# A feed-forward whose panels begin with a product made in two column pieces

## The reference, cut to what matters

```python
def swiglu(x, w_gate, w_up, w_down):
    return (jax.nn.silu(x @ w_gate) * (x @ w_up)) @ w_down

h = h + 0.5 * swiglu(rmsnorm(h, ffn1_norm[l]), ffn1_w_gate[l], ffn1_w_up[l], ffn1_w_down[l])
h = h + hybrid_mixer(rmsnorm(h, mix_norm[l]), ...)
h = h + 0.5 * swiglu(rmsnorm(h, ffn2_norm[l]), ffn2_w_gate[l], ffn2_w_up[l], ffn2_w_down[l])
```

## Time and profile before

| what | value |
|---|---|
| median of 3 runs (lowest, highest) | 2210.49 us (2203.68, 2211.15) |
| profiled execution | 2210.91 us |
| its span | 2209.1 us |
| PE busy | 2198.0 us, 99%, 18114 matmuls |
| PEld busy | 2180.8 us, 99%, 18114 loads |
| DVE busy | 1602.4 us, 73% |
| ACT busy | 1276.6 us, 58% |
| DMA | 386.68 MB, mean 175 GB/s |

### The profile page before, as it was taken

One profiled execution on the slowest core, in us unless ns is written; L12 is line 12 of the kernel. 1 busy time (PEld: TensorE's weight loads), 2 busy tenths in 40 slices (PEclk: granted clock), 3 DMA queues, 4 the chain that ended last, 5 costly groups with the idle time before them and its releaser, 6 DMA issues.

```text
span 2209.1 us, 48942 instructions
## 1 busy us (share of the span) xinstructions
PE 2198.0 (99%) x18114; PEld 2180.8 (99%) x18114; DVE 1602.4 (73%) x2450; ACT 1276.6 (58%) x1988; POOL 282.1 (13%) x328
## 2 busy tenths in 40 slices
PE   8999999999999999999999999999999999999999
PEld 8999999999999999999999999999999999999999
DVE  6655997665566579887768767888768766777775
ACT  6444786544444368766546646876556645565662
POOL 0001661100100136220020012010010010101000
PEclk9999999999999999999999999999999999999999
DMA  6555435555455544455555555355556645445553
GB/s 229 174 188 165 159 122 170 167 171 195 155 173 183 179 161 144 144 185 186 190 169 193 195 183 163 124 178 194 195 181 200 219 162 177 161 162 194 188 200 124
DMA packets 100408, 386.68 MB, mean 175 GB/s; under 512 B 11312, under 2 KB 12464, under 8 KB 100304
## 3 DMA queue, kind: packets, MB, share of 16 engines
q1 hardware_dynamic: 99648, 383.89, 52.2%
q0 software_dynamic: 368, 1.26, 0.2%
q10 hardware_dynamic: 288, 0.12, 0.0%
HBM read 384.18 MB, written 1.05 MB: 174 GB/s over the span
## 4 chain that ended last, share of the span: by engine, by line
PE 98%; ACT 1%; DVE 1%; issue 0%; DMA 0%; ACTq 0%
PE bank L387 16%; PE bank L389 15%; PE bank L388 15%; PE bank L395 15%; PE bank L396 14%; PE bank L397 14%; PE bank L759 1%; PE bank L1049 1%; PE bank L1050 1%; PE bank L1051 1%; PE bank L1096 0%; PE bank L709 0%; PE bank L740 0%; PE bank L940 0%; PE bank L943 0%; PE bank L942 0%
## 5 line engine op out<-in xcount | busy, mean ns | idle before, releaser
L412 DVE TENSOR_TENSOR wlo<-raw,whi 128x1024 fp32r<-128x1024 f32 (+1 forms) x677 | 893.3, 1322 | 177.8 <-ACT whi L405 165.4
L405 ACT ACTIVATE whi<-raw 128x1024 fp32r<-128x1024 f32 (+1 forms) x677 | 745.5, 1112 | 164.5 <-PE bank L389 117.2
L387 PE MATMUL bank<-u,whi 128*128 128x272 f32 (+1 forms) x1888 | 549.0, 291 | 7.1 <-DVE u L450 7.1
L389 PE MATMUL bank<-u,wlo 128*128 128x272 f32 (+1 forms) x1888 | 543.7, 288 | 0.0
L388 PE MATMUL bank<-u,whi 128*128 128x272 f32 (+1 forms) x1888 | 541.9, 287 | 0.0
L395 PE MATMUL bank<-u,whi 128*128 128x256 f32 x1888 | 529.2, 280 | 0.2
L397 PE MATMUL bank<-u,wlo 128*128 128x256 f32 x1888 | 527.4, 279 | 0.0
L396 PE MATMUL bank<-u,whi 128*128 128x256 f32 x1888 | 527.4, 279 | 0.0
L387 PEld LDWEIGHTS bank<-u,whi 128*128 128x128 f32 x1888 | 356.9, 189 | 8.0 <-DVE wlo L412 7.3
L388 PEld LDWEIGHTS bank<-u,whi 128*128 128x128 f32 x1888 | 357.0, 189 | 0.9 <-issue 0.2
L397 PEld LDWEIGHTS bank<-u,wlo 128*128 128x128 f32 x1888 | 357.6, 189 | 0.0
(11 more groups left out here) (332 smaller groups left out, 3448.8 us busy)
## 6 DMA issues: line engine op xcount, KB each, us to landing
raw<-w SPq DMA_DIRECT2D x552, 512.0 KB, 3.4
raw<-w SPq DMA_DIRECT2D x128, 704.0 KB, 4.1
h<-xT SPq DMA_DIRECT2D x4, 272.0 KB, 4.9
outT<-h SPq DMA_DIRECT2D x8, 128.0 KB, 4.7
consts<-cst POOLq DMA_DIRECT2D x1, 576.0 KB, 4.6
dist<-cst POOLq DMA_DIRECT2D x1, 192.0 KB, 2.7
rdist<-cst POOLq DMA_DIRECT2D x1, 192.0 KB, 3.0
sgain<-small POOLq DMA_DIRECT2D x1, 145.5 KB, 4.8
```

Source lines behind the costliest of these rows:

```text
L387: pe.matmul(out, w_h, x_hi, start=first, stop=False)
L389: return pe.matmul(out, w_l, x_hi, start=False, stop=last)
L405: act.activation(whi[:, n % RING, 0:COLS[n]], raw[:, n % RING, 0:COLS[n]], ACT.Copy).then_inc(hi_ready, 1)
L412: dve.tensor_tensor(wlo[:, n % RING, 0:COLS[n]], raw[:, n % RING, 0:COLS[n]], whi[:, n % RING, 0:COLS[n]], ALU.subtract).then_inc(lo_ready, 1)
```

## The change: what it does

In the gate and up panels of the five feed-forwards with 256 tokens, the first matmul of a panel (k = 0, high by high) is made as two, over columns 0 to cut and cut to 256, with the same weights. The first piece has `start=True`, the second has not. `CUTS` gives the column for each j of a step and each phase. For y = 5 and j = 0 it is 0, and there the matmul stays whole. Nothing else is changed: the columns that are computed, the banks, the waits and all other engines' instructions are the same.

```diff
+CUTS = {5: (0, 128, 64, 192), 7: (224, 32, 240, 16), 9: (248, 8, 252, 4), 10: (208, 48, 96, 160),
+        12: (250, 244, 254, 220)}
...
-        def split_products(pe, out, slot, k, x_hi, x_lo, first, last):
+        def split_products(pe, out, slot, k, x_hi, x_lo, first, last, cut=0):
...
-            pe.matmul(out[:, 0:SEQ], w_h, x_hi, start=first, stop=False, skip_group_check=True)
+            if cut:
+                pe.matmul(out[:, 0:cut], w_h, x_hi[:, 0:cut], start=first, stop=False, skip_group_check=True)
+                first = False
+            pe.matmul(out[:, cut:SEQ], w_h, x_hi[:, cut:SEQ], start=first, stop=False, skip_group_check=True)
...
                                 mm = split_products(pe, bank[g % 4], n % RING, k, u_at(uy, 0, k),
-                                                 u_at(uy, 1, k), k == 0, k == KD - 1)
+                                                 u_at(uy, 1, k), k == 0, k == KD - 1,
+                                                 CUTS[y][j] if k == 0 else 0)
```

## The result

The changed kernel takes 2221.09 us (median of 4 runs, 2220.36 to 2221.74). The kernel before, in the same comparison, takes 2207.09 us (2203.68 to 2211.15). The ratio is 1.0064, with a 95% interval of 1.0044 to 1.0083: slower, by 0.6%. Two of the four runs of before lie at 2203.68 us and two at 2210.49 and 2211.15, so its median falls between two levels; against the upper one, where the profiled execution lies, the change costs 10 us. I had forecast 2242 us. The profiled execution took 2220.83 us where that of before took 2210.91, so the two traces have 9.9 us between them to explain; 31.2 were forecast. The direction was right, the size was three times too large.

The account below looks back on a forecast made before the run. PE was taken to bound the kernel, with matmuls and weight loads busy for 99% of the span. The sum was 2210.9 + 22.5 (pairs) + 8.7 (pitch) = 2242 us, range 2220 to 2250.

Parts of the forecast that it names:

- (1) Number: In the five feed-forwards' gate and up panels, 209 split panels add 209 matmuls and 209 weight loads.
- (2) Price of a pair: Per split panel, two pieces take 2 x 0.112 us against 0.118 for one wide matmul: +0.106, 22.5 us in all.
- The load rows: Profile rows of narrow matmuls in rt: one weight load every 0.11 us, read as the pace of any narrow piece.
- rivals C and D: C, chance 0.04: second piece's load skipped or hidden, 2220 us; D, 0.03: also fast pitch in slow feed-forwards, 2190 us.
- (3) The pitch behind the pieces: In the five feed-forwards, pieces set the pitch anew, 0.85 of the matmuls at the slow one: +8.7 us.
- seven passages: Places in rt behind narrow matmuls; six of seven ran slow, from which the slow share of 0.85 was taken.
- rival B: Pieces turn nearly every panel of the five feed-forwards to the fast pitch, 2212.5 to 2221 us; chance 0.11.
- (4) Waits: At the split panels no wait is added or moved; the bank's handover 0.11 us later is hidden by three others.
- Rival E: Pieces cost their price but each feed-forward keeps its pitch, 2233 us; chance 0.27 together with mixtures of pitch.

## Why the prediction was wrong

What bounds the kernel: right. PE never waits, and every ns per matmul shows in the total; all twelve runs agree with it.

(1) Number: right, 18323 matmuls.

(2) Price of a pair: forecast 0.106 us each and 22.5 us in all; measured 24.9 in the trace and 0.115 us each in the run with 220 more pairs. The load rows gave the right mechanism: the width of a piece doesn't matter and equal weights are loaded again. It was 10% low: I had set two pieces at 112 ns each against one wide matmul at 118, but in the fast stream two at 113 stand against one at 113, and behind some cuts come a few matmuls of transition. So rivals C and D, which need the load skipped or hidden, fall. The Trainium skill, page TensorE: Matmul & The Clock Gate, section Back-to-back issue gap, says that in a stream of weight loads and matmuls both set the time from one matmul to the next, and gives about 81 ns for 128 columns and 131 ns for 512. The traces agree that the load counts, as 4 columns take 113 ns, but not with the figures: 128 columns take 111 ns, and 512 columns in rt (L1049 to L1051) start about 230 ns apart.

(3) The pitch behind the pieces: this step failed. I forecast +8.7 us and the runs showed -14.1: 20% of the feed-forward matmuls are at the slow pitch (1056 + 528 of 7920) where I took 85%. I had seen rightly that there are two pitches, what each is worth, and that pieces turn them and the stream keeps them. I took the share from seven passages as if they were seven draws. Four of them were one piece of code, L1082: six matmuls of 256 columns, 118 ns apart each time, and then six of 128, which is nearer to one observation than to four. I had left out the five norms, which set the pitch too, three slow and two fast. And the run with cut 8 shows that the way of a turn depends on what ran ahead. With a share of 0.5 for want of knowledge the sum would have been 22.5 - 3.5 = 19, 2230 us, and the range down to all fast, 2212, should have had more than the 0.11 of rival B. B is what happened: it was to lie at 2212.5 to 2221. That 2221.09 still falls above 2220, where I let the range begin, owes to the part of B that I let in and to the pairs that cost 2.4 us more than forecast; it isn't to the credit of this step.

(4) Waits: right, none was seen.

Rival E, each keeps its pitch, is refuted at y = 5 and 7. That the times of the kernel before are 7 us apart because one feed-forward differs was offered as a possibility; the traces show that y = 7 can fall either way at its norm, and that is as far as it is shown. Single runs lay at four levels, 2203.5, 2210.7, 2218 and, once, 2224.7 us, so if the steps are feed-forwards, y = 7 alone can't make them all.

What stays open is which feed-forwards make the 7 us steps of the kernel before, what the state is, what decides the way at a norm, and why no piece turned the 272 columns. The runs show that one matmul in two pieces is enough to turn the stream and that feed-forward and panel don't decide the way. They don't show the mechanism, and whether the timing of the other engines or of the loads from memory bears on it was not tested.

## What to carry to other kernels

Where PE bounds and a window shows another count of the same matmuls than the next, ask what stood between: it may be a state that one odd matmul can turn, worth 4% of every matmul behind it, and then it is enough to turn it once. Try the turn and count behind it: here a cut at 128 was right in all five places and a cut at 8 in three. Don't split a matmul for its own sake: in this format a piece costs a whole weight load, whatever its width. And passages that repeat one piece of code from one state are a single observation.

## What the runs showed of the hardware that I had not expected

An fp32r matmul of 256 columns at full granted clock takes 113.33 or 117.78 ns and keeps that over more than 1500 others, through loop ends and into the first panel of the next phase. Two pieces of 8 columns and 248 turn either into the other; a whole extra matmul did not, in any of five places. A matmul of 4 columns costs as much as one of 256. The fp32 matmuls of a norm can end it: y = 10 was entered slow and left fast, y = 12 entered fast and left slow, and behind the final norm either pitch was found. The single times of the kernel before lie in steps of about 7 us (2203.5, 2210.7, 2218, 2224.7); with one split at 128 in each feed-forward eight runs lay within 1.2 us.
